# Token sums for two feed-forward norms, a split spatial product and an earlier table load in a two-block transformer kernel

## The reference, cut to what matters

```python
for layer in range(2):
    xn = rms_norm(h, norm_mix[layer])
    if layer == 0:                       # "even": gated convolution and pooling
        h = h + einsum(mix_even(xn), w_out_even)
    else:                                # "odd": chunked spatial gating
        proj = gelu(xn @ w_in_odd, approximate=False)
        u, v = proj[..., :1024], proj[..., 1024:]
        vn = rms_norm(v, sgu_norm)       # reshaped to 4 chunks x 128 tokens x 8 heads x 128
        gate = einsum('hts,bnshc->bnthc', w_spatial * tril, vn) + b_spatial
        h = h + (u * gate) @ w_out_odd
    hn = rms_norm(h, norm_ffn[layer])
    g = causal_dwconv3(hn @ w_gate, conv_w) + conv_b
    h = h + (silu(g) * (hn @ w_up)) @ w_down
return rms_norm(h, final_norm)
```

## Time and profile before

| what | value |
|---|---|
| time, median of 3 runs | 1773.49 us (1772.46 to 1774.18) |
| time of the profiled execution | 1773.05 us |
| its span | 1771.4 us |
| TensorE matmul busy | 1724.3 us (97%) |
| TensorE weight load busy | 1429.1 us (81%) |
| VectorE, ScalarE, GpSimd busy | 960.5, 775.5, 421.5 us |

### The profile page before, as it was taken

How to read it: one execution, slowest core, us unless ns; L and a number is a source line. 1 busy time by engine, 2 the same in 40 slices (tenths; PEclk the granted TensorE clock), 3 DMA queues, 4 the chain that set the end, 5 groups by cost and what they waited for, 6 DMA issues and landing times.

```text
span 1771.4 us, 25386 instructions
## 1 busy us (share of the span) xinstructions
PE 1724.3 (97%) x8460; PEld 1429.1 (81%) x8460; DVE 960.5 (54%) x1751; ACT 775.5 (44%) x1374; POOL 421.5 (24%) x556
## 2 busy tenths in 40 slices
PE   7999999999999999799999999999999999999998
PEld 6788879899878888588878888888788788888886
DVE  6677767777763334675455555333346555555232
ACT  6666766666652233323343333222363433333222
POOL 4555665655520001300211111011003211111000
PEclk9999999999999999899999999999999999999999
DMA  4112123333223334123333333333332333333332
GB/s 136 51 45 62 47 54 80 77 79 82 76 64 97 98 107 124 55 83 99 92 96 95 95 95 95 114 98 98 95 95 63 92 95 95 95 95 92 97 95 84
DMA packets 284312, 154.39 MB, mean 87 GB/s; under 512 B 12655, under 2 KB 278770, under 8 KB 284242
## 3 DMA queue, kind: packets, MB, share of 16 engines
q1 hardware_dynamic: 281858, 148.95, 29.3%
q0 software_dynamic: 2336, 4.47, 1.1%
q10 hardware_dynamic: 48, 0.07, 0.0%
HBM read 147.02 MB, written 2.16 MB: 84 GB/s over the span
## 4 chain that ended last, share of the span: by engine, by line
PE 79%; DVE 10%; issue 5%; ACT 4%; POOL 1%; DMA 0%; ACTq 0%; DVEq 0%; POOLq 0%
PE ps L362 65%; PE ps L2426 2%; PE ps L974 2%; DVE tmp L1317 1%; DVE arena_r L1322 1%; PE ps L803 1%; PE ps L824 1%; PE ps L837 1%; ACT tmp L1045 1%; PE ps L785 1%; DVE ps L1309 1%; ACT w_split L305 1%; PE ps L674 1%; DVE stats L1314 1%; DVE tmp L1374 1%
## 5 line engine op out<-in xcount | busy, mean ns | idle before, releaser
L362 PE MATMUL ps<-u,w_split 128*128 128x512 f32 x3825 | 914.4, 397 | 10.4 <-DVE u L2006 7.3
L362 PEld LDWEIGHTS ps<-u,w_split 128*128 128x128 f32 x3825 | 717.4, 189 | 174.6 <-DVE u L2006 6.9
L321 DVE TENSOR_TENSOR w_split<-w_raw,w_split 128x1024 fp32r<-128x1024 f32 (+1 forms) x221 | 268.2, 1213 | 435.1 <-ACT w_split L305 435.0
L305 ACT CAST w_split<-w_raw 128x1024 fp32r<-128x1024 f32 (+4 forms) x321 | 289.0, 914 | 420.4 <-PE ps L362 385.6
L362 PE MATMUL ps<-arena_r,w_split 128*128 128x512 f32 x1824 | 417.5, 390 | 3.1 <-DVE arena_r L2566 1.7
L362 PEld LDWEIGHTS ps<-arena_r,w_split 128*128 128x128 f32 x1824 | 341.8, 188 | 76.1 <-DVE arena_r L2566 3.2
L2346 POOL TENSOR_TENSOR tmp<-tmp 128x512 f32<-128x512 f32 x44 | 57.1, 1297 | 425.8 <-ACT tmp L2331 425.8
L319 POOL TENSOR_TENSOR w_split<-w_raw,w_split 128x256 fp32r<-128x256 f32 x168 | 122.6, 760 | 24.4 <-ACT w_split L305 24.4
L1855 POOL TENSOR_TENSOR tmp<-tmp 128x512 f32<-128x512 f32 x40 | 56.9, 1422 | 269.5 <-ACT tmp L1814 234.5
L974 PE MATMUL ps<-u,w_split 128*128 128x264 f32 x768 | 105.8, 287 | 1.7 <-DVE arena_r L1342 1.7
L1045 ACT ACTIVATE tmp<-ps,stats 128x144 f32<-128x144 f32 (+3 forms) x128 | 69.3, 542 | 75.7 <-DVE stats L1309 73.4
(11 more groups left out here) (266 smaller groups left out, 1600.5 us busy)
## 6 DMA issues: line engine op xcount, KB each, us to landing
w_raw<-in_w_in_dram SPq DMA_DIRECT2D x118, 256.0 KB, 3.2
w_raw<-in_w_ffn_gate_dram SPq DMA_DIRECT2D x88, 256.0 KB, 3.1
w_raw<-in_w_ffn_up_dram SPq DMA_DIRECT2D x88, 256.0 KB, 3.1
w_raw<-in_w_ffn_down_dram SPq DMA_DIRECT2D x64, 256.0 KB, 3.1
w_raw<-in_w_in_even_dram SPq DMA_DIRECT2D x32, 256.0 KB, 3.1
w_raw<-in_w_in_odd_dram SPq DMA_DIRECT2D x32, 256.0 KB, 3.1
w_raw<-in_w_ffn_down_dram SPq DMA_DIRECT2D x32, 192.0 KB, 2.7
w_raw<-in_w_br_mla_dram SPq DMA_DIRECT2D x16, 256.0 KB, 3.1
```

The lines of the kernel that those rows point to most:

```text
L305: ins = act.copy(dst, src)
L321: ins = eng.tensor_tensor(lo, r, hi, ALU.subtract)
L362: last = pe.matmul(out_ap, w_tile(c, ws, k - n0), moving(k, ms), start=start and n == 0, stop=stop and n == len(total) - 1, skip_group_che ...
```

## The change

Three parts:

1. Both feed-forward norms take the second way. The squares of tiles 0 to 6 are summed on GpSimd, and the token sums of these stand between tiles 6 and 7 of the first gate product. Those of tile 7 stand behind tile 0 of the first up product, and the broadcast matmul behind tile 4 of it. ScalarE takes a root of 128 x 4 numbers, splits unit 2 of the stage high, and copies the broadcast to `rbc`; VectorE makes the diagonal. VectorE's first read of a gate result waits for that copy, and its low split of unit 2 stands behind this read, as before.
2. In the odd stage TensorE makes the spatial products of heads 0 to 3 ahead of the last u product, and those of heads 4 to 7 behind it. The steps of heads 0 to 3 on ScalarE and VectorE move ahead of the splits of m = 15.
3. The table load for the square root at the end (with a one-element activation) moves ahead of ScalarE's wait for the last product.

```diff
-            return tiles_before(tag) - (1 if tag != "out" else 0)
+            return tiles_before(tag) - sum(x in SHORT for x in NORMS[:NORMS.index(tag)])
...
+                        if tag == "down1" and last and j == 1 and m == per - 1:
+                            act.activation(rtok[:, 0:1], ones[:, 0:1], ACT.Sqrt)
                         act.wait_ge(sem("w_used"), num(c, i, 2 * per) + 1)
...
-                    if tag == "down1" and last and j == 1:
-                        act.activation(rtok[:, 0:1], ones[:, 0:1], ACT.Sqrt)
...
+        def pe_broadcast(pe, tag):
+            pe.wait_ge(sem("diagonal"), DIAGONALS.index(tag) + 1)
+            pe.matmul(bank(7), ones[:], sq[:, 0, :], start=True, stop=True).then_inc(sem("e_bc"), 1)
+
+        def act_token_rms(act, tag):
+            act.wait_ge(sem("summed"), norms_done(tag))
+            act.activation(sstok, bank(6, 0, NQ), ACT.Sqrt, scale=1.0 / D, bias=EPS).then_inc(sem("rms"), 1)
+
+        def act_broadcast_copy(act, tag):
+            act.wait_ge(sem("e_bc"), BROADCASTS.index(tag) + 1)
+            act.copy(rbc[:, 0, :], bank(7)).then_inc(sem("out_rsb"), 1)
...
                     if first and j == 0:
-                        pe_stats(pe, tag)
+                        product(pe, bank(j), c0 + j, u_real, range(KT - 1), stop=False, ready=h_ready(pe, tag))
+                        pe_token_sums(pe, tag, 6, False)
+                        product(pe, bank(j), c0 + j, u_real, (KT - 1,), start=False, ready=h_ready(pe, tag)) \
+                            .then_inc(sem("w_used"), 1)
+                    elif first and j == 1:
+                        product(pe, bank(j), c0 + j, u_real, (0,), stop=False)
+                        pe_token_sums(pe, tag, 6, True)
+                        product(pe, bank(j), c0 + j, u_real, (1, 2, 3, 4), start=False, stop=False)
+                        pe_broadcast(pe, tag)
+                        product(pe, bank(j), c0 + j, u_real, (5, 6, 7), start=False).then_inc(sem("w_used"), 1)
...
         def act_ffn(act, layer, tag):
             c0 = FIRST[("ffn", layer)]
-            act_stats(act, tag)
+            act_token_rms(act, tag)
+            act.wait_ge(sem("w_used"), c0 + 1)
+            w_hi(act, c0 + 2, 0, 4, "full")
+            act_broadcast_copy(act, tag)
...
         def dve_ffn(dve, layer, tag):
-            dve_stats(dve, tag)
+            dve.wait_ge(sem("rms"), norms_done(tag))
+            dve_token_diagonal(dve, tag)
...
                     dve.wait_ge(sem("w_used"), num(c, i, 4) + 1)
+                    if first and j == 0:
+                        dve.wait_ge(sem("out_rsb"), COPIES.index(tag) + 1)
...
-            for n in range(KT):
+            for n in range(KT - 1):
                 u_product(n)
-            for hd in range(C_HEADS):
+            for hd in range(C_HEADS // 2):
+                spatial(hd)
+            u_product(KT - 1)
+            for hd in range(C_HEADS // 2, C_HEADS):
                 spatial(hd)
...
             for m in range(2 * KT):
+                if m == 2 * KT - 1:
+                    for hd in range(C_HEADS // 2):
+                        y_hi(hd)
                 act.wait_ge(sem("w_used"), OV + m + 1)
...
             for m in range(1, 2 * KT):
+                if m == 2 * KT - 1:
+                    for hd in range(C_HEADS // 2):
+                        gated(hd)
+                        if hd >= 2:
+                            dve_gate_lo(dve, hd - 2)
+                    dve_gate_lo(dve, C_HEADS // 2 - 2)
+                    dve_gate_lo(dve, C_HEADS // 2 - 1)
                 w_lo(dve, OV + m + 2)
...
+            for hd in range(C_HEADS // 2, C_HEADS):
+                gated(hd)
+                if hd - 2 >= C_HEADS // 2:
                     dve_gate_lo(dve, hd - 2)
```

More of the change, by code:

```diff
@@ L1730, in tiles_before @@
             return KT * NORMS.index(tag)
+        SHORT = ("out", "eo", "oo", "down1")
         def acc_before(tag):
-            return tiles_before(tag) - (1 if tag != "out" else 0)
+            return tiles_before(tag) - sum(x in SHORT for x in NORMS[:NORMS.index(tag)])
         def hs_before(tag):
@@ L1847, in pool_squares @@
         def pool_squares(pool, tag):
-            for n in range(KT - 1 if tag in ("out", "down1") else KT):
+            for n in range(KT - 1 if tag in SHORT else KT):
                 pool.wait_ge(sem("squared"), tiles_before(tag) + n + 1)
@@ L2307, in body @@
                         pe.wait_ge(sem("ffn_g_read" if j % 2 == 0 else "ffn_a_done"), FT * layer + f - 1)
-                    product(pe, bank(j), c0 + j, u_real, ready=h_ready(pe, tag) if first and j == 0 else None) \
-                        .then_inc(sem("w_used"), 1)
                     if first and j == 0:
-                        pe_stats(pe, tag)
+                        product(pe, bank(j), c0 + j, u_real, range(KT - 1), stop=False, ready=h_ready(pe, tag))
[8 more added lines that the diff above has]
+                        product(pe, bank(j), c0 + j, u_real, (5, 6, 7), start=False).then_inc(sem("w_used"), 1)
+                    else:
+                        product(pe, bank(j), c0 + j, u_real).then_inc(sem("w_used"), 1)
             loop(pe, FT // 2, body)
@@ L2323, in body @@
                     act.wait_ge(sem("w_used"), num(c, i, 4) + 1)
-                    w_hi(act, c + 2 + i * 4) if last and j else w_hi(act, c + 2, i, 4, "full")
+                    if not (first and j == 0):
+                        w_hi(act, c + 2 + i * 4) if last and j else w_hi(act, c + 2, i, 4, "full")
                     act.wait_ge(sem("ffn_g_read"), FT * layer + f + 1)
@@ L2514, in dve_odd, with gated @@
                     .then_inc(sem("wst"), 1)
-            for m in range(1, 2 * KT):
+            def gated(hd):
+                y = y_bufs[hd % 4]
+                dve.wait_ge(sem("sgu"), hd + 1)
+                if hd == 2:
+                    dve.wait_ge(sem("ws_lo"), NQ)
+                    dve.wait_ge(sem("ws_hi"), NQ)
+                if hd >= 4:
+                    dve.wait_ge(sem("gate_lo"), hd - 3)
+                dve.scalar_tensor_tensor(out=y.rearrange("p (t n) -> p t n", t=NQ),
+                                         in0=bank(4 + hd % 4).rearrange("p (t n) -> p t n", t=NQ),
+                                         scalar=vcol("sgu_g", hd),
+                                         in1=bbc[:, :, hd * P:(hd + 1) * P].to_broadcast([P, NQ, P]),
+                                         op0=ALU.mult, op1=ALU.add).then_inc(sem("gate"), 1)
+            for m in range(1, 2 * KT):
+                if m == 2 * KT - 1:
[5 more added lines that the diff above has]
+                    dve_gate_lo(dve, C_HEADS // 2 - 1)
                 w_lo(dve, OV + m + 2)
```

22 lines of the change are left out of this document (7 added, 15 removed).

## The result

The changed kernel takes 1779.83 us (median of 6 runs, 1779.07 to 1782.90) against 1773.97 (6 runs, 1772.46 to 1774.18): +5.9 us, a ratio of 1.0038 (1.0027 to 1.0048). The ratios and their intervals here are estimates over all runs, not quotients of two medians. The kernel is slower by some 0.4%, an interval clear of no change, and 1779.83 is inside the forecast range of 1775 to 1784. The profiled execution has a span of 1777.8 us, 6.4 above the 1771.4 of before.

A forecast was written before the change was run, and what follows sets the result against it. TensorE's matmul stream, busy 97% of the span, was taken as the bound. Norms +1.3, odd-stage order +1.8, clock +5.3 and table load -0.7 sum to +7.7 on 1773.05; with the median 0.44 higher, 1781.2 us, range 1775 to 1784.

The forecast's parts named there:

- one wait for the last quarter of the spatial weights: Odd stage, head 0: TensorE waits 3.0 us until 1331.37, and the granted clock falls to 0.50 behind it.
- the low clock: Odd stage, behind the gap: granted clock of 0.50 for 4 to 9 us, until well into the last u product.
- the wait on unit 2: Each feed-forward start: TensorE still waits 0.6 us on unit 2's low split, begun behind the first gate read.
- the last square: End of kernel: the square begins as soon as the add ends, 0.7 us closer to the last product's end.
- Part 2 without the clock: Odd stage: the new order alone puts the residual product's last tile at 1352.9, +1.8 us (bounds +0.5 to +2.6).
- The clock: Odd stage: fall to 1.2 GHz costs 3.3 us in narrow matmuls and 2.0 in the last u product, +5.3 (0 to 7.8).
- The narrow matmuls: Odd stage, heads 0 to 3: 39 matmuls slow from 0.114 to about 0.2 us each, +3.3 us (0 to 4.4).
- Norms: Both feed-forward starts: two sum groups and the path to unit 2's split cost +0.65 a layer, +1.3 us (1.0 to 1.6).
- The table load: End of kernel: load leaves the path and the square starts earlier, -0.7 us (at most -0.76, at least 0).
- The clock did not stay: Rival for the odd stage: clock stays at 2.4 GHz, sum +2.4, 1775.9 us, no change that can be told; chance 0.23.
- A fall in a feed-forward start: Rival: clock falls near the two sum groups too, one more stretch of 1.7 us, sum about 1783; chance 0.12.
- Not slower: Rival: last quarter ready by 1328.4, no gap or clock fall, odd stage -1.2, sum -0.6, 1772.9 us; chance 0.05.

The follow-up runs named there:

- e4_early_quarter: Changed kernel with all three parts, but the last quarter of the spatial weights made together with the third: 1772.33 us, ratio 0.9992 to the kernel before.
- e5_repeat_fill: Changed kernel with 12 matmuls of the last u product made ahead of head 0 and the whole product repeated later: 1776.44 us, ratio 1.0026.
- e2_odd_only: Kernel before with only the new order of heads and last u product in the odd stage: 1780.00 us, ratio 1.0041.
- e7_norms_low_first: Kernel before with only the norms part, VectorE's low split of unit 2 moved ahead of its wait for the broadcast copy: 1770.24 us, ratio 0.9993.
- e8_norms_one_sum: Kernel before with only the norms part, unit 2's low split moved earlier and one group of token sums instead of two: 1769.84 us, ratio 0.9986.
- e3_table_only: Kernel before with only the table load moved ahead of ScalarE's wait for the last product: 1772.99 us, ratio 0.9999.
- e12_after_again: Changed kernel, unedited, profiled once more on the third chip: 1785.15 us in one run.
- e6_short_gap: Changed kernel with the last quarter of the spatial weights made ahead of the splits at m = 14: 1779.95 us, ratio 1.0038.
- e10_all_restart: Changed kernel with early quarter, earlier unit 2 low split, one sum group, and earlier gates of heads 4, 5 and high part of head 4: 1765.09 us, ratio 0.9962.

## Why the prediction was right, and where its sizes were off

- **Direction and mechanism.** Both are right: one wait for the last quarter of the spatial weights, then the clock. The wait, its releaser, the fall to 0.50 and the last tile's releaser are in the trace as forecast, e4_early_quarter takes away gap and clock together, e5_repeat_fill takes away the low clock and keeps the rest of the price, and both come close to what the prediction priced those pieces at. Of its other signs, the wait on unit 2 was 0.53 for 0.6; the low clock lasted some 10 us for "4 to 9", and the last square moved by 0.39 for 0.7.
- **Part 2 without the clock**, +1.8: measured +1.54 (e5_repeat_fill). From the start of head 0 to the quarter it took 1332.33 - 1328.27 = 4.06 for 3.97 forecast; GpSimd's restart 1351.08 - 1346.93 = 4.15, as forecast; from there to the last tile it took 7.36 for 7.4.
- **The clock**, +5.3: measured 4.84. The narrow matmuls cost 7.49 - 4.44 = 3.05 more for 3.3 forecast, since the clock fell about 1 us into them (in e2_odd_only, where it fell before, they cost 8.28 - 4.44 = 3.84). The last u product took 7.11 instead of 5.5, 1.6 more for 2.0. One of its grounds was thinner than it looked: the earlier trace rows shows one idle gap of 1.04 ahead of the low clock at 749.5, but the trace has two more close by, of 1.58 up to 740.17 and of 1.56 up to 745.11, so that row does not show how short a gap is enough. Scaling the narrow ones by the weight load, 189 to 329 ns, was the step with most at stake, and it held: from 0.114 each to a forecast of 0.2, measured 0.192 and 0.212.
- **Norms**, +1.3: measured +1.54, 0.77 a layer. The path forecast for unit 2 was 889.2 - 874.74 = 14.46, the trace has 14.59. Sums took 1.01 and 1.00 a group (880.73 - 879.72 and 882.99 - 881.99) where the prediction had 0.89, and the 18 wide matmuls behind them 3.90 where it had 4.12, so the two errors cancel: 885.63 - 879.72 = 5.91 for 5.90. The way from the broadcast to the first read was 1.98 for 1.91. No link of the path is wrong; the whole is 0.13 longer than forecast, and 0.77 lies within the "0.5" to "0.8" that the prediction gave for a layer. That the price is the split behind the read plus the second sum group is shown by e7_norms_low_first and e8_norms_one_sum.
- **The table load**, -0.7: measured -0.39 (1.45 to 1.06 from add to square). The term was mis-sized because the prediction took the square to begin as soon as the add ends. In e3_table_only, part 3 alone, 0.09 lies between them and the saving is 0.67, near the forecast; in the whole change 0.37 lies between them, of which the chain calls 0.33 issue. Why the two differ stays open. The drain that the Trainium skill, "ScalarE: Activation LUTs", "What ACT_TABLE_LOAD costs", puts behind a load shows in no trace here: moving the load saved less than its own 1.28, not more, and in the kernel before an activation follows the load of 509.53 at 510.82, 0.01 behind its end. (The saving that the prediction worked out from the page, an estimate, would be 0.7 + 1.38 = 2.1, not 2.0.)
- **What the sum didn't hold.** By these measurements it is 1.54 + 6.38 - 0.39 = +7.5, and the profiled pair differed by +6.4: layer 1 of the traced execution after happened to run at the quicker pace, 0.90 in the loop and 0.2 in the start. So the forecast of +7.7 against a median of +5.9 is not evidence of a wrong term. How near a median of six runs comes to it is in part luck, since unedited stretches move an execution by several us; that the parts alone also sum to +7.7 by their medians is as much luck.
- **Rivals.** The clock did not stay in either traced execution of this kernel (after, e12_after_again), and all six timed runs lie above that rival's 1775.9. What it would have cost shows in e5_repeat_fill, +1.5 for the odd stage. A fall in a feed-forward start did not come; the start is 51.1, or 50.9 at the quicker pace, wherever part 1 stands unmended. "Not slower" was priced at -1.2 for the odd stage with an early quarter; e4_early_quarter has -1.37.

## What to carry to other kernels

When work is moved ahead of a big product, list every operand of it and who makes each: the product was cover for the last one. A wait in TensorE's stream can cost more than its length if the clock falls behind it (here 2.9 us of idle time cost 1.5 with the new order, and the clock 4.8 more). Shortening it by 1.1 gave back 1.15; making it vanish gave back 116.99 - 109.24 = 7.75. And compare executions piece by piece at marks that both kernels have: two traces of the kernel before differed by 3.7 us here and two of the changed one by 5.7, while the odd stage repeated to 0.02 in each.

## What the hardware showed that I had not expected

- The clock fell behind a wait of 1.75 us in e6_short_gap, as behind one of 2.86. In both, TensorE does 128-column matmuls bound by weight loads before and after it. The same head stretch without idle time kept 1.00 (e4_early_quarter, e5_repeat_fill). In all four traces with the wait (after, e2, e6, e12) the clock, once it had fallen, stayed low through the rest of the narrow matmuls and rose inside the last u product, whose matmuls have 512 columns.
- It may fall inside the gap (e2_odd_only), 1 us behind it (after) or, by the stretch 1334 to 1337 at 0.76, nearly 2 us behind it (e6_short_gap). Between e2_odd_only and after, with the same gap, this is worth 1.1 us.
- The feed-forward loop holds one of two paces through a whole layer, 11.09 or 11.03 us a hidden tile, in unedited code; three executions (after, e3_table_only, e4_early_quarter) changed from the first to the second between layers. What sets it is open.
- A group of token sums in the stream of the feed-forward start took 1.01 and 1.00, where the one of the earlier trace rows took 0.89.
- The same GpSimd step took 1.28 us in one place and 2.20 beside VectorE's 128 x 1024 low split (e10_all_restart).
